# Seven block products in place of eight for the last eight chunks of an up projection

## The chip, the cores and the metric

The kernel runs on one core of a Trainium2 chip, as one program. The metric is device time in microseconds (us) of one execution. The engines are called as the profile calls them: PE (TensorE, the matmuls), PEld (its weight loads), DVE (VectorE), ACT (ScalarE), POOL (GpSimd) and SP (SyncE, which issues most transfers).

## The reference

Two transformer blocks over 512 tokens of width 1024, all in float32. The part around the change is the convolutional feed-forward of the first block:

```
def conv_ffn(x, w_up, conv_w, conv_b, w_down):
    u = causal_dwconv(x @ w_up, conv_w, conv_b)   # 3 taps along the tokens
    g, val = jnp.split(u, 2, axis=-1)             # 2 x 2816 columns
    return (jax.nn.gelu(g) * val) @ w_down
```

Before it stand a mixer and a cross attention, after it a second block with four mixers, an output projection (`out2`) and an MLP, `square(relu(h @ w1)) @ w2` (`m1` and `m2`, hidden width 4096).

## The kernel before

**Work.** Every large product is cut into chunks of one 128x1024 weight tile (512 KB). SP loads chunk after chunk into four stage buffers. Each chunk is split into a rounded part `whi` (ACT, line 1973) and a rest `wlo` (DVE, line 2491); the activations likewise into `xh` and `xl`. A product is then three matmuls: high times high, high times low, low times high. There are seven places for split chunks, so a split runs at most seven chunks ahead of its use.

**A plain up chunk** (`feat`, lines 1509 to 1511) makes 128 features for 512 tokens in one PSUM bank: 8 parts of the contraction x 3 matmuls of 512 columns, 24 matmuls. There are 44: gate and value of each of 22 feature tiles in turn. Behind each chunk ACT copies the bank into `U` (2234) and makes the last tap with bias from the bank (2237); DVE adds two taps (2863, 2866). Behind the gate's taps ACT makes the gelu (2241), behind the value's DVE multiplies the two into `hid1` (2874).

**Seven block products.** `down`, `m2` and the last 24 of 32 tiles of `m1` already use the seven products of a 2x2 block scheme: contraction, features and tokens are halved, and seven products of sums of quarters take the place of eight. In `m1` a group is four chunks' worth of features; its seven products are called, in their order, r2, t11, r1, r3, t12, r4, t22 (`M1_KINDS`). Each is 24 matmuls of 256 columns (1739 to 1741). Between them: after r2 ACT copies the bank away ("taken", 2063); after t11 DVE makes v, which t12 waits for; after r1 DVE makes w (3048) and ACT writes it back ("seed", 2067), which r4 waits for; after r3 DVE makes c22 and c21 (3052, 3054), and t22 waits for c21. Sums of the activations (r1, r2, r3) live in three of the seven places for split chunks (`keep`), given back (`give`) as the last group's r2, r1 and r3 are done. The sums of weight quarters are made in DRAM by transfers of 1 MB that POOL issues one after the other (`add_up`, from the list `ORDER`; `at(n)` names the chunk behind which the n-th may start).

**Order.** A planner (`Plan`) writes one list of steps; each engine takes its own steps out of it in that order, with semaphores between engines. `pump` emits splits until the places are full. Nothing on an engine's queue overtakes.

**The down stage** (`seven`, lines 1713 to 1715) begins with product 0, whose activations are in `first`; products 1 to 3 need x_from 1 to 3 (ACT 2012, DVE 2525), products 4 to 6 need x_from 4 to 6, emitted behind the last chunk's steps. Each product is 12 matmuls of 512 columns. In the last up chunk a semaphore `half` tells after half its matmuls that x_from 1 to 3 may overwrite `xh`.

The plan's loop over the up chunks, before:

```
        for j in self.feat("up", 2 * NF1):
            if j == 2 * NF1 - 1:
                self.seven_ahead("down")
            self.step("up", j // 2, j % 2)
            self.out(("up", j), "up_y", j + 1)
            if j % 8 == 7 and j < 8 * GROUPS["down"]:
                self.combine("down", "r1", j // 8)
                self.combine("down", "r3", j // 8)
            if j == 17:
                self.seven_first("down")
```

## Time and profile before

| | us |
|---|---|
| median of 3 runs | 1231.41 (1231.21 to 1232.08) |
| the profiled execution | 1231.81 |
| its span, first to last instruction | 1230.0 |
| PE busy in it | 1222.7 |
| DVE busy | 899.3 |
| ACT busy | 652.9 |
| last eight up chunks | 569.89 to 613.41 |
| the 42 block products of `m1` | 950.88 to 1071.83 |

Starts in rows are in us from the span's start. A matmul row's own length is a modelled one and overlaps the next; the distance between starts is what PE spends on it. The same holds for ACT and DVE, where an instruction starts a little before the one ahead of it has ended.

### The profile page before, as it was taken

How to read it: one execution, taken by the hardware profiler on the slowest of the kernel's cores; microseconds unless marked ns; L12 is line 12 of the kernel's file. 1: busy time of each engine (PE TensorE's matmuls, PEld its weight loads, DVE VectorE, ACT ScalarE, POOL GpSimd, SP SyncE). 2: the span in 40 equal slices, each digit the busy share in tenths (PEclk: the TensorE clock that was granted, in tenths of full speed). 3: DMA queues.
4: the chain of work that ended last, by engine and by line, in shares of the span. 5: the costliest groups of instructions: out<-in, count | busy, mean ns of one | idle time of the engine just before them, and what ended most of it. 6: DMA issues, size and time to landing. Idle time of an engine off the chain costs nothing.

```text
span 1230.0 us, 17180 instructions
## 1 busy us (share of the span) xinstructions
PE 1222.7 (99%) x6662; PEld 1050.5 (85%) x6662; DVE 899.3 (73%) x1281; ACT 652.9 (53%) x1078; POOL 56.0 (5%) x80
## 2 busy tenths in 40 slices
PE   9999999999999999999999999999999999999998
PEld 9887898898889888888888899778898999988886
DVE  6778888576568656555588587887687777887886
ACT  5565654244546444444465464669354544665654
POOL 0000012000000000000000000000000000000000
PEclk9999999999999999999999999999999999999999
DMA  8445478837635787878676429776736789776562
GB/s 296 150 139 192 161 265 226 283 116 210 185 107 188 209 236 208 198 241 202 212 246 181 139 69 259 207 194 191 248 104 159 265 271 265 256 220 190 173 213 78
DMA packets 63976, 244.53 MB, mean 199 GB/s; under 512 B 6900, under 2 KB 14580, under 8 KB 54424
## 3 DMA queue, kind: packets, MB, share of 16 engines
q1 hardware_dynamic: 53096, 167.55, 40.6%
q0 software_dynamic: 10368, 75.50, 24.9%
q8 instruction: 53, 0.87, 0.3%
q10 hardware_dynamic: 432, 0.39, 0.1%
q14 instruction: 27, 0.22, 0.1%
HBM read 235.55 MB, written 81.26 MB: 258 GB/s over the span
## 4 chain that ended last, share of the span: by engine, by line
PE 99%; DMA 0%; DVE 0%; ACT 0%; issue 0%; DVEq 0%
PE bank L1509 15%; PE bank L1510 15%; PE bank L1511 15%; PE bank L1713 6%; PE bank L1715 6%; PE bank L1714 6%; PE bank L1740 3%; PE bank L1741 3%; PE bank L1739 3%; PE bank L1654 2%; PE bank L1658 2%; PE bank L1653 2%; PE bank L1656 2%; PE bank L1655 2%; PE bank L1657 2%; PE bank L1790 1%
## 5 line engine op out<-in xcount | busy, mean ns | idle before, releaser
L2491 DVE TENSOR_TENSOR wlo<-stage,whi 128x1024 fp32r<-128x1024 f32 (+1 forms) x276 | 332.8, 1212 | 113.5 <-ACT whi L1973 112.4
L1509 PE MATMUL bank<-xh,whi 128*128 128x512 f32 (+1 forms) x944 | 339.4, 360 | 0.2 <-issue 0.2
L1510 PE MATMUL bank<-xl,whi 128*128 128x512 f32 (+1 forms) x944 | 335.5, 355 | 0.0
L1511 PE MATMUL bank<-xh,wlo 128*128 128x512 f32 (+1 forms) x944 | 335.5, 355 | 0.0
L1973 ACT CAST whi<-stage 128x1024 fp32r<-128x1024 f32 (+1 forms) x276 | 284.9, 1039 | 78.5 <-PE bank L1715 27.3
L1509 PEld LDWEIGHTS bank<-xh,whi 128*128 128x128 f32 x944 | 178.5, 189 | 29.9 <-issue 5.3
L1511 PEld LDWEIGHTS bank<-xh,wlo 128*128 128x128 f32 x944 | 178.5, 189 | 25.1
L1510 PEld LDWEIGHTS bank<-xl,whi 128*128 128x128 f32 x944 | 178.6, 189 | 24.4 <-issue 0.2
L1715 PE MATMUL bank<-whi,xl 128*128 128x512 f32 x328 | 127.7, 389 | 0.0
L1714 PE MATMUL bank<-wlo,xh 128*128 128x512 f32 x328 | 127.7, 389 | 0.0
L1713 PE MATMUL bank<-whi,xh 128*128 128x512 f32 x328 | 127.7, 389 | 0.0
L1715 PEld LDWEIGHTS bank<-whi,xl 128*128 128x128 f32 x328 | 61.6, 188 | 12.8
L1714 PEld LDWEIGHTS bank<-wlo,xh 128*128 128x128 f32 x328 | 61.6, 188 | 12.8
L1713 PEld LDWEIGHTS bank<-whi,xh 128*128 128x128 f32 x328 | 61.6, 188 | 12.7
L2863 DVE SCALAR_TENSOR_TENSOR R<-R,par 128x512 f32<-128x512 f32 x44 | 33.1, 752 | 53.2 <-ACT R L2237 53.2
L2234 ACT COPY R<-bank 128x512 f32<-128x512 f32 x44 | 25.8, 587 | 82.4 <-PE bank L1511 82.4
L2525 DVE TENSOR_TENSOR xl<-R,xh 128x512 fp32r<-128x512 f32 x92 | 61.7, 686 | 10.5 <-ACT xh L2012 9.6
L2012 ACT CAST xh<-R 128x512 fp32r<-128x512 f32 x70 | 42.4, 616 | 36.2 <-DVE R L3086 20.1
L1741 PE MATMUL bank<-xh,wlo 128*128 128x256 f32 x192 | 54.4, 283 | 0.0
L1739 PE MATMUL bank<-xh,whi 128*128 128x256 f32 x192 | 54.4, 283 | 0.0
L1740 PE MATMUL bank<-xl,whi 128*128 128x256 f32 x192 | 54.4, 283 | 0.0
L2915 DVE SCALAR_TENSOR_TENSOR R<-R,par 128x512 f32<-128x512 f32 x60 | 41.7, 746 | 1.6 <-ACT R L2280 1.3
(408 smaller groups left out, 2017.7 us busy)
## 6 DMA issues: line engine op xcount, KB each, us to landing
stage<-in_W_m SPq DMA_DIRECT2D x50, 512.0 KB, 4.2
stage<-in_W_up SPq DMA_DIRECT2D x44, 512.0 KB, 4.4
m_a<-in_W_m POOLq DMA_DIRECT2D x14, 1024.0 KB, 8.2
m_b<-in_W_m POOLq DMA_DIRECT2D x14, 1024.0 KB, 7.6
stage<-in_W_in_a SPq DMA_DIRECT2D x19, 512.0 KB, 4.4
stage<-in_W_down SPq DMA_DIRECT2D x18, 512.0 KB, 4.3
stage<-in_W_out SPq DMA_DIRECT2D x16, 512.0 KB, 5.3
m_c<-in_W_m POOLq DMA_DIRECT2D x7, 1024.0 KB, 6.1
```

Source lines behind the costliest of these rows:

```text
L1509: e.matmul(b[:, cols], hi[:, k, :], xh[:, k, cols], start=(k == 0), stop=False)
L1510: e.matmul(b[:, cols], hi[:, k, :], xl[:, k, cols], start=False, stop=False)
L1511: last = e.matmul(b[:, cols], lo[:, k, :], xh[:, k, cols], start=False, stop=(k == 7))
L1713: e.matmul(b[:], x[:, c], hi, start=new, stop=False, skip_group_check=True)
L1714: e.matmul(b[:], x[:, c], lo, start=False, stop=False, skip_group_check=True)
L1715: last = e.matmul(b[:], z[:, c], hi, start=False, stop=end, skip_group_check=True)
L1739: e.matmul(o, hi[:, k, w], x[:, k, :], start=(new and f == 0 and k == 0), stop=False, skip_group_check=True)
L1740: e.matmul(o, hi[:, k, w], z[:, k, :], start=False, stop=False, skip_group_check=True)
L1741: last = e.matmul(o, lo[:, k, w], x[:, k, :], start=False, stop=(k == 3), skip_group_check=True)
L1973: e.copy(whi[:, plan.place[i], 0:width(i)], stage[:, s, 0:width(i)]).then_inc(S["w_hi"])
L2491: e.tensor_tensor(wlo[:, plan.place[i], c], stage[:, i % NSTAGE, c], whi[:, plan.place[i], c].bitcast(F32), ALU.subtract).then_inc(S["w_lo"])
L2525: e.tensor_tensor(lo, source_of(name, k), hi.bitcast(F32), ALU.subtract).then_inc(S["x_lo"])
```

## The change

The last 8 of the 44 plain up chunks become two groups of seven block products (`UP_PLAIN` = 36, 50 chunks in all), with the code of `m1` made general (`feat_seven`, `feat_taken`, `feat_seed`, `feat_combine`). The convolution behind them works on two feature tiles at once: three quarters come by an ACT copy out of the banks (`up_quarter`), the fourth by c22; after r4 ACT makes the value's last tap (`up_y` 1), after t22 the gate's (`up_y` 0), from `U` in SBUF; DVE's taps for the value follow t22 (`up_taps` 1), and those for the gate, the gelus and the multiplications (`up_done`) follow the next group's r2, or t22 itself in the last group. Sums of `x` for r1 to r4 are made beside plain chunks 8 to 15 and 32 to 34 (and r4's rounding after the first r2), and three places are kept for them from chunk 32 on. The weight sums grow from 72 to 80 transfers, in another order of start, with the d sums of `m2` last. x_from 1 to 3 of `down` wait for the second last block product in place of `half`. Behind `out2`, one of two splits moves from ahead of the last tile's norm to behind the turn of tile 2.

```diff
+GROUPS = {"up": 2, "down": 4, "m1": 6, "m2": 8}
+UP_PLAIN = 2 * NF1 - 4 * GROUPS["up"]
+FEATS = {"up": [(kind, g) for g in range(GROUPS["up"]) for kind in M1_KINDS], "m1": M1_SEVEN}
+ORDER = [o for o in ORDER if (o[0], o[2][0]) != ("m2", "d")] + [o for o in ORDER if (o[0], o[2][0]) == ("m2", "d")]
...
             if t == 3:
                 self.used += 5
-                self.pump(2)
+                self.pump(1)
...
             if t >= 2:
                 self.turn(name, t - 1)
+            if t == 3:
+                self.pump(1)
...
-        for j in self.feat("up", 2 * NF1):
-            if j == 2 * NF1 - 1:
-                self.seven_ahead("down")
+        self.up_x = self.x
+        for j in self.feat("up", UP_PLAIN):
...
+            if 8 <= j < 12:
+                self.combine("up", ("t21", "t22", "t11", "t12")[j - 8])
+            elif 12 <= j < 16:
+                self.combine("up", ("r1", "r3", "r2", "r4")[j - 12])
+            elif j == 17:
                 self.seven_first("down")
+            elif UP_PLAIN - 4 <= j < UP_PLAIN - 1:
+                self.sum_kept("up", ("r2", "r1", "r3")[j - UP_PLAIN + 4])
+        for i, (kind, g) in enumerate(FEATS["up"]):
+            self.up_seven(i, kind, g)
...
+    def sum_kept(self, name, kind):
+        self.keep((name, kind))
+        self.step("x_sum", name, kind)
+        self.x_split(name, kind)
+
+    def feat_seven(self, name, i, kind, g, last):
+        if kind not in NEW_BANK:
+            self.fill(name, g, kind)
+        self.need()
+        self.step("seven_feat", name, i)
+        self.used += 1
+        if kind in ("r1", "r2", "r3") and g == last:
+            self.give((name, kind), "mm", CHUNK0[name] + PLAINS[name] + i + 1)
+
+    def up_seven(self, i, kind, g):
+        last = GROUPS["up"] - 1
+        self.feat_seven("up", i, kind, g, last)
+        if kind == "r2":
+            self.copy("up", "taken", g)
+            self.step("feat_taken", "up", g)
+            if g == 0:
+                self.step("x_sum", "up", "r4")
+                self.x_split("up", "r4")
+            else:
+                self.pump()
+                self.up_done(g - 1)
+        elif kind == "t11":
+            self.combine("up", "v", g)
+        elif kind == "r1":
+            self.combine("up", "w", g)
+            self.out(("up", g, "r1"), "combined", self.combined)
+            self.copy("up", "seed", g)
+            self.step("feat_seed", "up", g)
+        elif kind == "r3":
+            self.combine("up", "c22", g)
+            self.combine("up", "c21", g)
+        else:
+            if (kind, g) == ("t22", last):
+                self.seven_ahead("down")
+            n = ("t12", "r4", "t22").index(kind)
+            self.pump()
+            self.step("up_quarter", n, g)
+            self.out(("up", g, ("t11", "r2", "r3")[n]), "up_u", UP_PLAIN + 3 * g + n + 1)
+            if n:
+                self.step("up_y", g, 2 - n)
+            if n == 2:
+                self.step("up_taps", g, 1)
+                if g == last:
+                    self.up_done(g)
+        self.pump()
+
+    def up_done(self, g):
+        self.step("up_taps", g, 0)
+        self.step("up_gelu", g)
+        self.step("up_mult", g)
...
-                if name == "down" and k < 4:
-                    q.wait_ge(S["half"], 3)
-                elif name == "m2" and k < 4:
+                if name in SEVEN and k < 4:
                     q.wait_ge(S["mm"], CHUNK0[name] - 1)
...
+            def up_taps(g, r):
+                for i in range(2):
+                    c, u = UP_PLAIN // 2 + 2 * g + i, U[i][r]
+                    y, w = (hid1[:, c, :] if r else ygs[i]), 22 * r + c
+                    q.wait_ge(S["up_y"], UP_PLAIN + 4 * g + (1 if r else 3) + i)
+                    e.scalar_tensor_tensor(out=y, in0=u[:, 0:512], scalar=P("fcw", w), in1=y, op0=ALU.mult, op1=ALU.add
+                                           ).then_inc(own.inc())
+                    after()
+                    e.scalar_tensor_tensor(out=y, in0=u[:, 1:513], scalar=P("fcw", 44 + w), in1=y, op0=ALU.mult,
+                                           op1=ALU.add).then_inc(S["up_t" if r else "up_c"])
...
-                if n < 43:
-                    return CHUNK0["up"] + 2 + 8 * (n - 17) // 5
-                if n < 61:
-                    return CHUNK0["in2_c"] + 1 + (n - 43)
-                if n < 64:
-                    return CHUNK0["m1"] + 3 + 2 * (n - 61)
-                return CHUNK0["m1"] + PLAIN + 2 + 4 * (n - 64)
+                if n < 40:
+                    return CHUNK0["up"] + 2 + 3 * (n - 17) // 2
+                if n < 58:
+                    return CHUNK0["in2_c"] + 1 + (n - 40)
+                if n < 62:
+                    return CHUNK0["m1"] + 2 + 2 * (n - 58)
+                if n < 72:
+                    return CHUNK0["m1"] + PLAIN + 2 + 4 * (n - 62)
+                return CHUNK0["m2"] + 1 + 4 * (n - 72)
```

## Rows read from the trace of the kernel before

**Rows 1.** The page: PE's busy time, and the granted clock by fortieths of the span

```profile
PE 1222.7 (99%) x6662; PEld 1050.5 (85%) x6662; DVE 899.3 (73%) x1281; ACT 652.9 (53%) x1078; POOL 56.0 (5%) x80
...
PEclk9999999999999999999999999999999999999999
```

**Rows 2.** The longest wait of PE in the span: total, times, longest

```profile
PE bank L1952 <- DVE R L2564: 1.2, 1, 1.2
```

**Rows 3.** PE's timeline: first matmul of the stretches named in the prediction

```profile
569.89 0.39 PE L1509 MATMUL bank<-xh,whi 128*128 128x512 f32 x1
...
613.41 0.39 PE L1713 MATMUL bank<-whi,first 128*128 128x512 f32 x1
...
950.88 0.28 PE L1739 MATMUL bank<-whi 128*128 128x256 f32 x1
...
1071.83 0.40 PE L1713 MATMUL bank<-whi,first 128*128 128x512 f32 x1
```

**Rows 4.** Timeline of ACT, then of DVE, around plain up chunks

```profile
570.09 0.59 ACT L2234 COPY R<-bank 128x512 f32<-128x512 f32 x1 [0.58 <-PE bank L1511]
570.57 0.79 ACT L2237 ACTIVATE R<-bank,par 128x512 f32<-128x512 f32 x1
571.24 1.05 ACT L1973 CAST whi<-stage 128x1024 fp32r<-128x1024 f32 x1
578.47 0.63 ACT L2241 ACTIVATE R<-R 128x512 f32<-128x512 f32 x1 [1.68 <-DVE R L2866]
...
576.89 0.75 DVE L2863 SCALAR_TENSOR_TENSOR R<-R,par 128x512 f32<-128x512 f32 x1 [2.04 <-ACT R L2237]
577.68 0.75 DVE L2866 SCALAR_TENSOR_TENSOR R<-R,par 128x512 f32<-128x512 f32 x1
```

**Rows 5.** Timeline of ACT, then of DVE, in the last block group of `m1`

```profile
1055.23 2.00 ACT L1973 CAST whi<-stage 128x1024 fp32r<-128x1024 f32 x2
1061.23 0.59 ACT L2067 COPY bank<-R 128x512 f32<-128x512 f32 x1 [2.49 <-DVE R L3048]
...
1056.39 2.36 DVE L2491 TENSOR_TENSOR wlo<-stage,whi 128x1024 fp32r<-128x1024 f32 x2 [0.73 <-ACT whi L1973]
1060.51 0.69 DVE L3048 TENSOR_TENSOR R<-R,bank 128x512 f32<-128x512 f32 x1
1065.18 0.68 DVE L3052 TENSOR_TENSOR R<-R,bank 128x512 f32<-128x512 f32 x1
1065.78 0.69 DVE L3054 TENSOR_TENSOR bank<-bank,R 128x512 f32<-128x512 f32 x1
```

**Rows 6.** Timeline of ACT, then of DVE, where `down` begins

```profile
612.59 1.66 ACT L2012 CAST xh<-R 128x512 fp32r<-128x512 f32 x3
...
619.05 0.68 DVE L2525 TENSOR_TENSOR xl<-R,xh 128x512 fp32r<-128x512 f32 x1
```

**Rows 7.** DMA issues of 612 to 622 us, then the page's: KB, us to landing

```profile
stage<-down_c SPq DMA_DIRECT2D x1, 512.0 KB, 3.2
stage<-in_W_down SPq DMA_DIRECT2D x1, 512.0 KB, 3.4
...
stage<-in_W_up SPq DMA_DIRECT2D x44, 512.0 KB, 4.4
```

**Rows 8.** Windows, busy us by engine: the last up chunks, a group of `m1`

```profile
569.86:613.41 43.55, 43.55 (x194) 36.06 (x193) 24.62 (x29) 20.89 (x30) 3.00 (x5) 1.00 0.75 217
950.90:971.00 20.10, 20.10 (x169) 20.10 (x168) 15.87 (x20) 11.79 (x15) 1.07 (x2) 1.00 0.76 246
```

**Rows 9.** POOL's timeline: the last sums issued beside the up chunks

```profile
569.62 0.81 POOL L3317 DMA_DIRECT2D m_c<-m_a  x1 [9.32 <-DMA m_b<-in_W_m]
578.57 0.83 POOL L3317 DMA_DIRECT2D m_d<-m_c  x1 [8.14 <-DMA m_c<-m_a]
```

**Rows 10.** ACT's timeline at the last tile of `out2`

```profile
899.91 2.00 ACT L1973 CAST whi<-stage 128x1024 fp32r<-128x1024 f32 x2
904.90 0.60 ACT L2413 ACTIVATE R<-bank 128x512 f32<-128x512 f32 x1 [2.99 <-PE bank L1658]
```

More of the change, by code:

```diff
@@ L1139, in m1_seven @@
+    def up_done(self, g):
+        self.step("up_taps", g, 0)
+        self.step("up_gelu", g)
+        self.step("up_mult", g)
+        c = UP_PLAIN // 2 + 2 * g + 2
+        if c % 4 == 0 and c <= 4 * GROUPS["down"]:
+            self.combine("down", "r1", c // 4 - 1)
+            self.combine("down", "r3", c // 4 - 1)
+    def m1_seven(self, i, kind, g):
+        self.feat_seven("m1", i, kind, g, NF2 // 4 - 1)
         if kind == "r2":
             self.copy("m1", "taken", g)
-            self.step("m1_taken", g)
+            self.step("feat_taken", "m1", g)
@@ L1377, in build_program @@
         hid2 = tiles(reg(16, NF2 * 512), NF2)
-        rs = {"down": [tiles(reg(60 + 2 * g, 512), 2) for g in range(4)],
+        rs = {"down": [tiles(reg(kb, 512), 2) for kb in (60, 62, 92, 94)],
               "m2": [tiles(reg(92 + 2 * g, 512), 2) for g in range(2)]
@@ L1460, in build_program, with feat_x @@
         turned = [nc.dram_tensor(f"turned{u}", (128, 1024 if u % 4 else 512), F32, kind="Internal").ap() for u in range(8)]
[L1462 removed]
+        def feat_x(name, kind, lo):
             if kind in ("r1", "r2", "r3"):
[L1464 removed]
+                return tiles((wlo if lo else whi)[:, plan.kept[name, kind][0], :], 4)
             k, c = X_T["t21" if kind == "r4" else kind]
@@ L1521, in feat @@
                 ks = {None: range(8), "front": range(4), "back": range(4, 8)}[part]
-                if (name, j) in LAST_X.values():
-                    by_weights(b, i, cols, range(4)).then_inc(S["half"])
-                    ks = range(4, 8)
                 last = by_weights(b, i, cols, ks)
@@ new lines, in x_sum, with feat_taken @@
+                e.copy(feat_x(name, kind, 0), raw_of(SUM_AT[kind])).then_inc(S["x_hi"])
+            def feat_taken(name, g):
+                q.wait_ge(S["mm"], CHUNK0[name] + PLAINS[name] + FEATS[name].index(("r2", g)) + 1)
+                if name == "up":
+                    if g >= 2:
+                        q.wait_ge(S["combined"], plan.combined_at["up", "c21", g - 2])
+                    else:
+                        q.wait_ge(S["x_lo"], plan.x_at["up", "r3"])
+                e.copy(feat_v[name][:, g % 2, :], bank_of(name, g, "r2")[:]).then_inc(S["taken"])
@@ new lines, in feat_seed, with up_quarter @@
+            def feat_seed(name, g):
+                q.wait_ge(S["combined"], plan.combined_at[name, "w", g])
+                e.copy(bank_of(name, g, "r2")[:], feat_w[name][:, g % 2, :]).then_inc(S["taken"])
+            def up_quarter(n, g):
+                q.wait_ge(S["mm"], CHUNK0["up"] + UP_PLAIN + FEATS["up"].index((("t12", "r4", "t22")[n], g)) + 1)
+                q.wait_ge(S["up_t" if n == 1 else "up_c"], UP_PLAIN // 2 + 2 * g)
+                e.copy(u_of(("t11", "t12", "t21")[n]), tiles(bank_of("up", g, ("t11", "r2", "r3")[n])[:], 2)).then_inc(S["up_u"])
@@ new lines, in up_y @@
+            def up_y(g, r):
+                q.wait_ge(S["up_u"], UP_PLAIN + 3 * g + 3 - r)
+                if r:
+                    q.wait_ge(S["combined"], plan.combined_at["up", "c22", g])
+                else:
+                    q.wait_ge(S["up_h"], UP_PLAIN // 2 + 2 * g)
+                    q.wait_ge(S["x_lo"], plan.x_at["up", "r4"])
+                for i in range(2):
+                    c = UP_PLAIN // 2 + 2 * g + i
+                    e.activation(hid1[:, c, :] if r else ygs[i], U[i][r][:, 2:514], ACT.Identity, bias=P("fcb", 22 * r + c),
+                                 scale=P("fcw", 88 + 22 * r + c)).then_inc(S["up_y"])
@@ L2069, in m1_quarter, with up_gelu @@
+            def up_gelu(g):
+                for i in range(2):
+                    q.wait_ge(S["up_c"], UP_PLAIN // 2 + 2 * g + i + 1)
+                    e.activation(ygs[i], ygs[i], ACT.Gelu_apprx_tanh).then_inc(S["up_g"])
             def m1_quarter(n, g):
-                q.wait_ge(S["mm"], CHUNK0["m1"] + PLAIN + M1_SEVEN.index((("t12", "r4", "t22")[n], g)) + 1)
+                q.wait_ge(S["mm"], CHUNK0["m1"] + PLAIN + FEATS["m1"].index((("t12", "r4", "t22")[n], g)) + 1)
                 e.activation(t_of("m2", ("t11", "t12", "t21")[n], g), tiles(bank_of("m1", g, ("t11", "r2", "r3")[n])[:], 2),
@@ L3044, in m1_combine @@
                     e.tensor_tensor(v, v, b1, ALU.subtract).then_inc(S["combined"])
                 elif kind == "w":
-                    q.wait_ge(S["mm"], done + M1_SEVEN.index(("r1", g)))
-                    q.wait_ge(S["combined"], plan.combined_at["m1", "v", g])
+                    q.wait_ge(S["mm"], done + FEATS[name].index(("r1", g)))
+                    q.wait_ge(S["combined"], plan.combined_at[name, "v", g])
+                    if name == "up" and g >= 2:
+                        q.wait_ge(S["taken"], plan.copied_at["up", "seed", g - 2])
@@ L3056, in m1_last, with up_mult @@
+            def up_mult(g):
+                for i in range(2):
+                    c = UP_PLAIN // 2 + 2 * g + i
+                    q.wait_ge(S["up_t"], c + 1)
+                    q.wait_ge(S["up_g"], c + 1)
+                    e.tensor_tensor(hid1[:, c, :], ygs[i], hid1[:, c, :], ALU.mult).then_inc(S["up_h"])
             def m1_last(g):
```

150 lines of the change are left out of this document (75 added, 75 removed).

## The prediction

> **What bounds the kernel now.** I read the page first: PE is busy 1222.7 us of 1230.0 and its granted clock is full in all forty slices [rows 1]. Next the waits of PE: the longest of all is 1.2 us, at the start [rows 2]. So the time is the sum of the matmuls, and any other engine counts only when it makes PE wait; the reader should then look for how near the others are to that. The windows say it: in a group of m1's block products DVE is busy 15.87 of 20.10 us, ACT 11.79 [rows 8]. The timelines give each instruction's pace [rows 4 to 6], and it is these that decide here.
>
> **What PE saves.** Eight plain up chunks last from 569.89 to 613.41, 43.52 us, 5.44 a chunk, 0.2267 a matmul of 512 columns. m1's 42 block products last from 950.88 to 1071.83, 120.95 us, so 2.88 each, 0.120 a matmul of 256 columns [rows 3]. Two groups are 14 x 2.88 = 40.32 us: PE saves **3.20 us** (0.26%), if nothing makes it wait.
>
> A rule of the Trainium skill gives another price (TensorE: Matmul & The Clock Gate, "Wait — 56ns, not 53.3ns?"): a warm matmul costs its columns at 2.4 GHz plus about 2.5 ns. By it the saving would be an estimated 192 x 215.8 - 336 x 109.2 ns = 4.7 us, and my result 1.5 us lower; these rows pay some 13 ns beyond the columns, so the row's price stands.
>
> **What stands between the products.** Paces, start to start. DVE: a wlo 1.14 (two end 2.36 after the first begins, one lasts 1.22), an addition of 512 columns 0.60 (1065.18 to 1065.78) [rows 5], a tap 0.79 (576.89 to 577.68) [rows 4]. ACT: a whi 0.95 [rows 5], a bank copy 0.48 to 0.50, a last tap 0.67 (570.57 to 571.24) [rows 4], an x cast 0.52 (three in 1.66) [rows 6]. Hand-over: 0.20 from PE's last matmul to ACT [rows 3, 4], 1.16 from a whi's start to its wlo's, 0.72 from w to the seed [rows 5], 0.79 from the last tap to the gelu (577.68 to 578.47) and, by its 0.63 length, 0.66 from gelu to multiplication (an estimate) [rows 4].
>
> A group asks of DVE 7 wlo (7.98), v, w, c22, c21 (2.40), 8 taps (6.32) and 2 multiplications (1.20): 17.9 us of 20.16, where the last eight plain chunks left it busy 24.62 of 43.55 [rows 8]. On average that fits. The order decides whether it fits in time. I follow both queues from the first block product (0 = its start), with products at 2.88.
>
> *First group.* v is ready at 7.9 (due 11.5, when t12 starts), c21 at 13.8 (due 17.3). PE doesn't wait. But ACT can take the last quarter only after t22, and the value's taps stand on DVE behind t22's wlo, though their inputs are ready by then.
>
> *Second group, from 20.16.* The eleventh split's whi starts at 20.39 (ACT has just ended the value's last taps), its wlo at 21.55. DVE has stood idle from 19.8. Value taps 22.69 to 25.85. Then r2's step: as r2's place is given back, two splits are due, to 28.13; then the four gate taps to 31.29; the first multiplication; the second waits for the second gelu, 31.95; v starts at 32.54 and ends at 33.2. t12 was due at 11 x 2.88 = 31.68: **PE 1.6 late**. Then wlo 33.14, w 34.28, seed 35.00. r1 gives back another place, so two more splits, which on ACT stand behind the seed: whi at 35.5, wlo 36.7 and 37.8, c22 38.96, c21 39.56 to 40.25. t22 would start at 39.05 now: **another 1.3**. down starts at 43.2, not 40.32.
>
> *Start of down.* r3's two splits and t12's, r4's follow on ACT. The load into a stage buffer is issued when the wlo four chunks earlier is done, here 37.9, and takes 3.2 to 3.4 us alone, 4.4 in the middle of the up stage [rows 7]. So that whi starts at 41.2 to 42.4; behind it a quarter's copy, a whi, a copy and two last taps, then x_from 1 at 45.5 to 46.7, whose DVE part ends 1.35 later. down's product 1 is due at 45.9: **1.0 to 2.2**. x_from 4 has more ahead of it on DVE: x_from 1 to 3, a wlo, eight taps and two multiplications with a gelu between: it is ready 2.6 after product 4 is due: **2.6**. Behind it DVE needs 1.74 to 2.35 a product (wlo, x, at times a sum) against 2.72, so it catches up. Before the change the same x_from 4 ended at 619.7, 4.6 ahead of its product at 613.41 + 4 x 2.72 [rows 3, 6].
>
> Sum of waits: 6.5 with the fastest loads, 7.7 with the slowest. I take 3.5 us a load, nearer the lone ones, since no sum is left then (below): **6.8 us**.
>
> A bound from below, with no idling on DVE at all from 21.55: eleven wlo 12.5, sixteen taps 12.6, eleven additions 6.6, and x_from 4's own 0.69 are 32.4, so 54.0 at best, due 40.32 + 10.88 = 51.2. At least 2.8 us are lost by DVE's work alone. From above: all four waits with loads of 4.4.
>
> That DVE and ACT don't overtake is what all this rests on. The Trainium skill says the same (TensorE page, "Architectural detail": both are strict FIFO queues).
>
> **The other edits.** (a) Sums of x: 8 operations of DVE of 1024 columns beside plain chunks 8 to 15, and three casts and three subtractions beside 32 to 34, one per 5.44 us chunk, where DVE has more than 2 us free [rows 8]; no splits are due while three places go. Nothing; without that cover about 1.2 each. (b) x_from 1 to 3 freed by the second last product instead of `half`: the permission comes 2.88 ahead of down, as early as half a chunk was; nothing by itself. (c) Sums in DRAM: one in about 9 us (569.62 to 578.57) [rows 9], and 23 now want to start beside the plain chunks, one in 8.2 us; they run late, by some 20 us into the first group, and slow loads that are four products ahead. Nothing; for m2 each d sum starts 20 to 29 chunks ahead of its use. If one came late, PE would wait for its 9 us transfer. (d) out2: the second split stood in 2.99 us in which ACT waited for PE [rows 10], and its chunk is used three half chunks (8.6 us) and more later. PE waits in neither place [rows 2]: nothing, from a loss of 1 us at most if the split is late. (e) The last tap is read from SBUF rather than from PSUM: up to 0.13 a piece less on ACT, 0.3 in all on the chain to x_from 1.
>
> **Result.** Profiled execution: 1231.81 - 3.20 + 6.8 = 1235.4, with 1.8 outside the span as now. It stands 0.4 above the median of the runs, so the median becomes **1235.0 us**, slower by 0.29%. Without the third and fourth of its waits it would be 1231.1; own range 1233.5 to 1236.
>
> **Rivals.** (1) *DVE is late but never idle, the loads and ACT never in the way*: 2.8 us lost, 1231.0, the same. For it: the fit on average; against it: every idle stretch above is a wait for a whi that stands behind something. (2) *DVE keeps up*: faster, 1228.2. This is so if x_from 4 is ready by 51.2 and c21 by 37.4, that is if the taps find the idle stretches, such as that from 19.8 to 21.5 in which the value's taps could begin. It needs a DVE order other than I read from the plan. For it: m1's groups have no wait, with 2.5 us to spare at the last c21 (1066.5 against 41 x 2.88 + 950.88 = 1068.96) [rows 3, 5]; against it: up adds 6.3 us of taps in front of v. (3) *PE's clock drops in the waits*: every granted clock is full here, the longest idling 1.2 us [rows 1, 2]; one wait of 2.6 is longer than the trace shows. At 1.2 GHz a down product takes 5.44; three of them add 8 us, of which later waits hide a part: about 1240. The skill's page on TensorE ("What's actually happening") holds that the clock is released by activity and throttled by idling, which would make such a wait dearer; no row here shows it. (4) *The sums of m2's d come late*: 1240 or more.
>
> **Chances.** Forecast 0.55; (1), with values up to 1233.9 in which part of the waits is gone, 0.23; (2) 0.13; (3) 0.06; (4) 0.03. A measurement of this kernel tells 0.2% (2.5 us) from no change. Slower by more 0.63, within 0.24, faster 0.13. The range reaches from rival 1, a little below, to past the slowest loads with something for the clock: 1230.3 to 1237.5.
>
> **What the profile would show.** Right: PE's waits of 1.6 and 1.3 us in the second group, on DVE's v and c21, and of 1 to 3 us on x_from 1 and 4 in down, none in the first group; 2.88 a product; DVE with eight taps ahead of x_from 4. Wrong: a PE without waits there, taps in another place, or a granted clock below full after 600 us.

## The result, and the profile after

The changed kernel takes 1242.85 us (median of 5 executions, 1241.48 to 1244.55) against 1231.41 before: a ratio of 1.0093 [1.0081, 1.0104], slower by a little under 1%, clear of the noise. The profiled execution has a span of 1241.6 us, 11.6 more than before. The forecast was 1235.0: its sign was right, its size some 8 us too small.

The page of the changed kernel, PE's busy time and the clock by fortieths. In the forty slices little shows; PE's digit is 8 in two slices where it was 9, and the clock's digit, 9 for anything from 90% up, is the same:

```profile
PE 1223.8 (99%) x6806; PEld 1056.1 (85%) x6806; DVE 922.7 (74%) x1307; ACT 663.5 (53%) x1090; POOL 61.5 (5%) x88
...
PE   9999999999999999999899999999999999899998
...
PEclk9999999999999999999999999999999999999999
```

The waits of PE from 565 us on (total, times, longest), where the kernel before had none over 0.2:

```profile
PE bank L1779 <- DVE wlo L2583: 3.8, 1, 3.8
PE bank L1779 <- DVE xl L2617: 2.1, 1, 2.1
PE bank L1804 <- DVE bank L3157: 1.7, 2, 1.0
PE bank L1779 <- issue: 1.6, 1, 1.6
PE bank L1804 <- DVE R L3139: 1.3, 1, 1.3
```

PE's timeline has the places. L1804 to L1806 are block products by features (up, m1), L1779 to L1781 those of down and m2, L3139 is v, L3157 c21:

```profile
601.05 0.28 PE L1806 MATMUL bank<-whi,wlo 128*128 128x256 f32 x1
602.65 0.36 PE L1804 MATMUL bank<-xh,whi 128*128 128x256 f32 x1 [1.32 <-DVE R L3139]
...
608.36 0.28 PE L1806 MATMUL bank<-xh,wlo 128*128 128x256 f32 x1
609.65 0.36 PE L1804 MATMUL bank<-xh,whi 128*128 128x256 f32 x1 [1.02 <-DVE bank L3157]
...
617.07 0.47 PE L1779 MATMUL bank<-whi,xh 128*128 128x512 f32 x1 [1.57 <-issue]
...
625.12 0.39 PE L1781 MATMUL bank<-whi,xl 128*128 128x512 f32 x1
627.57 0.47 PE L1779 MATMUL bank<-whi,xh 128*128 128x512 f32 x1 [2.06 <-DVE xl L2617]
...
628.44 0.63 PE L1779 MATMUL bank<-whi,xh 128*128 128x512 f32 x1
628.87 0.63 PE L1780 MATMUL bank<-wlo,xh 128*128 128x512 f32 x1
...
631.43 0.48 PE L1780 MATMUL bank<-wlo,xh 128*128 128x512 f32 x1
```

A wait costs more than its bracket says: from start to start less the usual pitch (0.12 and 0.227), the four cost 1.48, 1.17, 1.73 and 2.22, in all 6.60. Each is followed by one interval that is some 0.08 too long (602.65 to 602.84), in all 0.3. Behind the last, ten intervals take 3.86 us (627.57 to 631.43) instead of 2.27: another 1.6. The windows show why: the clock of that stretch was for the most part at the lower of its two levels, 1.2 GHz. The second window has the wait of 3.8 us that ends at 1084.45, and behind it the same happens again, for another 1.6 us:

```profile
628.00:632.00 4.00, 4.00 (x13) 3.10 (x12) 3.07 (x6) 3.94 (x6) 0.00 (x0) 0.57 0.00 0
...
1080.00:1095.00 15.00, 11.20 (x42) 8.76 (x42) 14.31 (x20) 10.36 (x16) 0.54 (x1) 0.89 0.76 271
```

By stage, first matmul to first matmul, with the marks of [rows 3]: PE reaches the first block product 0.39 earlier (569.50), all of which lies ahead of the up stage and differs from execution to execution (the first up chunk starts between 380.2 and 382.1 in the profiles of this case). Up's end takes 43.09 instead of 43.52. From down's first product (612.59) to the first of m1's blocks (955.86) it is 343.27 instead of 337.47, 5.80 more, all of it in down. m1's blocks take 121.88 instead of 120.95, m2 up to its last matmul 157.81 instead of 152.12 (1223.95 before, 1235.55 after). The sum of the five differences is the 11.6.

So there are two sites. One is where I looked: +5.4 net at the second group and down's start, of which 1.6 is the clock. The other, +6.6, is the end of m1 and the start of m2, where I had priced the moved sums at nothing: 0.9 at the last t22 (a wait of 0.71), 4.0 at m2's product 1 (products are counted from 0) and 1.6 of clock behind it.

At the first site, ACT waits twice for a load ahead of x_from 1 (the profile names no releaser for PE's wait at product 1; the first xl of x_from 1 ends at 616.97, just ahead of 617.07). Then DVE makes eight taps and two multiplications between a wlo and the xl of x_from 4:

```profile
610.40 1.05 ACT L2038 CAST whi<-stage 128x1024 fp32r<-128x1024 f32 x1 [1.72 <-DMA stage<-down_a]
612.65 1.05 ACT L2038 CAST whi<-stage 128x1024 fp32r<-128x1024 f32 x1 [0.71 <-DMA stage<-down_c]
...
618.34 1.23 DVE L2583 TENSOR_TENSOR wlo<-stage,whi 128x1024 fp32r<-128x1024 f32 x1 [0.17 <-ACT whi L2038]
619.48 0.75 DVE L3164 SCALAR_TENSOR_TENSOR R<-R,par 128x512 f32<-128x512 f32 x1
...
626.74 0.68 DVE L2617 TENSOR_TENSOR xl<-R,xh 128x512 fp32r<-128x512 f32 x1
```

ACT's timeline at the second site, in the changed kernel:

```profile
1066.41 1.05 ACT L2038 CAST whi<-stage 128x1024 fp32r<-128x1024 f32 x1 [4.20 <-DMA stage<-m_d]
1069.41 0.59 ACT L2136 COPY bank<-R 128x512 f32<-128x512 f32 x1 [1.96 <-DVE R L3145]
1069.94 2.94 ACT L2038 CAST whi<-stage 128x1024 fp32r<-128x1024 f32 x3
1077.91 1.05 ACT L2038 CAST whi<-stage 128x1024 fp32r<-128x1024 f32 x1 [5.02 <-DMA stage<-m_b]
```

ACT stands in a split and waits for its load, longer than any product lasts. POOL's timeline names what the loads share the DMA with. Two of m2's sums run there, and a third is issued at 1080.95; the last sum before the change was issued at 1037.73:

```profile
1054.46 0.83 POOL L3440 DMA_DIRECT2D m_b<-in_W_m  x1 [10.89 <-PE bank L1806]
1066.21 0.81 POOL L3440 DMA_DIRECT2D m_c<-m_a  x1 [10.92 <-DMA m_b<-in_W_m]
```

DMA issues from 1048 to 1085 us (KB each, median us to landing), the kernel before first, without a sum in flight from about 1048 on:

```profile
stage<-m_a SPq DMA_DIRECT2D x4, 512.0 KB, 3.8
stage<-m_c SPq DMA_DIRECT2D x3, 512.0 KB, 4.3
stage<-m_b SPq DMA_DIRECT2D x3, 512.0 KB, 4.7
stage<-m_d SPq DMA_DIRECT2D x1, 512.0 KB, 3.1
```

and the kernel changed:

```profile
stage<-m_b SPq DMA_DIRECT2D x3, 512.0 KB, 5.9
stage<-m_a SPq DMA_DIRECT2D x3, 512.0 KB, 7.0
stage<-m_c SPq DMA_DIRECT2D x3, 512.0 KB, 6.9
m_b<-in_W_m POOLq DMA_DIRECT2D x1, 1024.0 KB, 11.3
...
stage<-m_d SPq DMA_DIRECT2D x1, 512.0 KB, 9.5
```

The loads from `in_W_m` in the same stretch went from 3.9 to 4.9. No load waited for its sum: from 1050 us on the only thing for which SP held a weight load back was a stage buffer, that is the wlo that frees it (total, times, longest):

```profile
SPq L3301 <- DVE wlo L2583: 138.1, 59, 6.2
```

### The profile page after: what moved, and what is told of

The parts are those of the page before. It is cut to its first block, busy times and chain, and to the rows that moved or that the text cites. A ratio compares the mean times of both kernels' runs of the same rounds, so it can differ in the third digit from the quotient of the medians.

```text
span 1241.6 us, 17554 instructions
## 1 busy us (share of the span) xinstructions
PE 1223.8 (99%) x6806; PEld 1056.1 (85%) x6806; DVE 922.7 (74%) x1307; ACT 663.5 (53%) x1090; POOL 61.5 (5%) x88
## 4 chain that ended last, share of the span: by engine, by line
PE 93%; DVE 2%; DMA 2%; ACT 1%; issue 1%; DVEq 0%; ACTq 0%
PE bank L1578 14%; PE bank L1579 13%; PE bank L1580 13%; PE bank L1779 6%; PE bank L1780 6%; PE bank L1781 6%; PE bank L1806 3%; PE bank L1805 3%; PE bank L1804 3%; PE bank L1720 2%; PE bank L1724 2%; PE bank L1721 2%; PE bank L1719 2%; PE bank L1723 2%; PE bank L1722 2%; DVE wlo L2583 1%
## 5 line engine op out<-in xcount | busy, mean ns | idle before, releaser
L1578 PE MATMUL bank<-xh,whi 128*128 128x512 f32 (+1 forms) x880 | 314.2, 357 | 0.2 <-issue 0.2
L1579 PE MATMUL bank<-xl,whi 128*128 128x512 f32 (+1 forms) x880 | 310.3, 353 | 0.0
L1580 PE MATMUL bank<-xh,wlo 128*128 128x512 f32 (+1 forms) x880 | 310.2, 353 | 0.0
L1578 PEld LDWEIGHTS bank<-xh,whi 128*128 128x128 f32 x880 | 166.3, 189 | 27.5 <-issue 5.3
L1580 PEld LDWEIGHTS bank<-xh,wlo 128*128 128x128 f32 x880 | 166.3, 189 | 22.8
L1779 PE MATMUL bank<-whi,xh 128*128 128x512 f32 x328 | 129.2, 394 | 7.4 <-DVE wlo L2583 3.8
L1781 PE MATMUL bank<-whi,xl 128*128 128x512 f32 x328 | 129.0, 393 | 0.0
L1779 PEld LDWEIGHTS bank<-whi,xh 128*128 128x128 f32 x328 | 62.3, 190 | 21.7 <-issue 4.4
L1804 PE MATMUL bank<-xh,whi 128*128 128x256 f32 x256 | 72.7, 284 | 3.0 <-DVE bank L3157 1.7
L1781 PEld LDWEIGHTS bank<-whi,xl 128*128 128x128 f32 x328 | 62.2, 190 | 13.1
L1805 PE MATMUL bank<-xl,whi 128*128 128x256 f32 x256 | 72.4, 283 | 0.0
L1806 PE MATMUL bank<-xh,wlo 128*128 128x256 f32 x256 | 72.4, 283 | 0.0
L2955 DVE SCALAR_TENSOR_TENSOR R<-R,par 128x512 f32<-128x512 f32 x36 | 27.0, 751 | 37.9 <-ACT R L2328 37.9
L1805 PE MATMUL bank<-wlo,whi 128*128 128x256 f32 x192 | 54.3, 283 | 0.0
```

The costliest lines, as they stand in the source:

```text
L1578: e.matmul(b[:, cols], hi[:, k, :], xh[:, k, cols], start=(k == 0), stop=False)
L1579: e.matmul(b[:, cols], hi[:, k, :], xl[:, k, cols], start=False, stop=False)
L1580: last = e.matmul(b[:, cols], lo[:, k, :], xh[:, k, cols], start=False, stop=(k == 7))
L1779: e.matmul(b[:], x[:, c], hi, start=new, stop=False, skip_group_check=True)
L1781: last = e.matmul(b[:], z[:, c], hi, start=False, stop=end, skip_group_check=True)
L1804: e.matmul(o, hi[:, k, w], x[:, k, :], start=(new and f == 0 and k == 0), stop=False, skip_group_check=True)
```

## The experiments

Fifteen kernels ran; each ratio is against the kernel before on the same chip. Theory one: the end of m1 is the sums' timetable alone. Theory two, for the first site: only the order of DVE's queue is at fault, since on average the work fits. Its rival: the work itself is too much there.

### The sums respaced

Eight sums beside m1's block groups as before the change, the rest later in m2.

```diff
-                if n < 72:
+                if n < 70:
                     return CHUNK0["m1"] + PLAIN + 2 + 4 * (n - 62)
-                return CHUNK0["m2"] + 1 + 4 * (n - 72)
+                if n < 72:
+                    return CHUNK0["m2"] + 3 + 4 * (n - 70)
+                return CHUNK0["m2"] + 11 + 3 * (n - 72)
```

> The changed kernel with another timetable of the weight sums alone: beside m1's block groups only the first 8 of the 10 sums (the last behind product 30 instead of 38 of them), the two others and the d sums of m2 during m2. Theory: the changed kernel loses at two places independent of each other; the second, at the end of m1 and the start of m2, comes from loads of 7 to 9.5 us beside sums of m2 while splits fall due in pairs. So the waits of 0.7 and 3.8 us there and the slow matmuls behind them go, the places in up and down stay: 1242.85 - 6.6 = 1236.2 us (1235.5 to 1237.5). Rival: the waits there come from elsewhere (later phase after the stall in down, the split moved behind out2): 1241 to 1244.

Measured: 1236.26 us (1.0045 [1.0028, 1.0062]), span 1233.5. Both waits of the second site are gone, the four of the first stand (1.4, 1.0, 1.6, 2.1), and 0.4 is new at down's product 16. As expected by theory one, the median is 6.6 us lower. Of the profiles, m1's blocks are back at 120.95 and m2 is at 152.55, together 6.2 us less; the profiled span is 8.1 less, as here the clock also stayed full behind the wait of 2.06 at product 4:

```profile
627.00:631.00 4.00, 4.00 (x19) 3.32 (x18) 3.06 (x5) 3.81 (x6) 0.00 (x0) 1.00 0.15 59
```

### The kernel before, with its sums late

```diff
+ORDER = [o for o in ORDER if (o[0], o[2][0]) != ("m2", "d")] + [o for o in ORDER if (o[0], o[2][0]) == ("m2", "d")]
...
                 if n < 64:
-                    return CHUNK0["m1"] + 3 + 2 * (n - 61)
-                return CHUNK0["m1"] + PLAIN + 2 + 4 * (n - 64)
+                    return CHUNK0["m1"] + PLAIN + 2 + 4 * (n - 54)
+                return CHUNK0["m2"] + 1 + 4 * (n - 64)
```

(with the sums ahead of these spread over the earlier stages so that 54 are out when m1's groups begin)

> The kernel before with the late timetable alone: 72 sums, no block groups in up, the m2 d sums last, 10 sums beside m1's block groups up to behind product 38 and 8 beside m2. Theory: the place at the start of m2 shows in it too, with waits on wlo there and none in up and down: 1231.4 + 6.6 = 1238 us (1234 to 1239.5; how long a load takes beside a sum depends on where the two meet). Rival (the new place is a consequence of the block groups in up): 1231.4, no wait.

Measured: 1238.51 (1.0059 [1.0044, 1.0075]), span 1235.3. Its two waits from 540 us on, in m1's last group and in m2's start:

```profile
PE bank L1710 <- DVE wlo L2488: 3.1, 1, 3.1
PE bank L1736 <- DVE bank L3051: 0.3, 1, 0.3
```

No block product in up, and a wait in the same place (m2's product 1), with the same slow clock behind it: the second site needs no group in up. Theory one is shown from both sides. Which of the moved sums does it, the last two beside m1's groups or the first beside m2, these two kernels don't separate.

### DVE's order, on top of the change and with the sums respaced

v, w and the seed moved ahead of the first group's last taps (a); the last group's taps moved behind down's products 1 and 3 (b).

```diff
+            if g:
+                self.up_done(g - 1)          # (a) in r1's step, no longer in r2's
...
-                self.step("up_taps", g, 1)
-                if g == last:
-                    self.up_done(g)
+                if g < last:
+                    self.step("up_taps", g, 1)
...
+            if name == "down" and i == 1:    # (b)
+                self.step("up_taps", GROUPS["up"] - 1, 1)
+            if name == "down" and i == 3:
+                self.up_done(GROUPS["up"] - 1)
```

Both, with the sums of the change:

> The changed kernel with another order of the vector queue alone: in the second up group v, w and the seed stand ahead of the first group's gate taps, gelus and multiplications, and the last group's taps, gelus and multiplications stand behind down's products 1 and 3 instead of ahead of x_from 4. Theory: the four waits in up and down and the slow clock behind them go, so that place gives the 3.2 us of the matmuls instead of taking 5.4: 1242.85 - 8.6 = 1234.2 us (1233 to 1236.5). Rival (the vector engine's sum of work, or the loads, hold PE up whatever the order): at least 2.8 us of waits stay there, 1237 or more.

Both, with the sums respaced:

> Both together: the timetable of the first experiment and the order of the third. Theory: no wait at either place, the matmuls' saving is all that is left: 1231.4 - 3.2 = 1228.2 us (1227.8 to 1229.5). Rival (work or loads hold PE up whatever the order): 1231 or more.

(b) alone and (a) alone, with the sums respaced:

> The kernel changed, with the two summing transfers respaced as in the first experiment (that one took 1236.3) and only the last group's four-tap sets moved behind down's products 1 and 3; v and w stay where the change has them. DVE's work is only moved to a later due time. If DVE has no slack there (the theory now): the wait at product 4 (2.06) goes, the waits at t12 and t22 (1.36, 1.02) stay, and a new wait of 2 to 4 us stands at the 17th product of down (about 660 us): 1236 to 1238. If the order is what costs: product 4's wait goes and nothing takes its place, 1233.5.

> The kernel changed, with the respaced sums, and only v, w and the seed of a group moved ahead of the first group's last taps, gelu and product. If DVE's work is what is short: the wait at t12 (1.36) goes, those of t22, x_from 1 and product 4 grow by about as much in all, 1235 to 1237, with no new wait at 660 us. If the order is what costs: 1234.9.

Measured: 1244.94, 1238.50, 1239.58 and 1241.52 us (ratios 1.0107, 1.0059, 1.0066, 1.0063; the last between 1.0036 and 1.0090). The first compares with the changed kernel's 1242.85, the other three with the respaced sums' 1236.26: no median is better, though with (a) alone the median hides a gain (below). The waits of the second one:

```profile
PE bank L1781 <- DVE R L3215: 4.3, 1, 4.3
PE bank L1781 <- issue: 1.5, 1, 1.5
PE bank L1806 <- DVE bank L3159: 1.1, 1, 1.1
```

The waits at t12 and at product 4 are gone, as they should be, and a new one of 4.3 us stands at 661 us, down's product 16, on v of down (L3215). It comes with (b) alone too, at the same 4.3. DVE's timeline just ahead of it shows a queue that does nothing but its regular work and never gets ahead:

```profile
655.16 1.23 DVE L2585 TENSOR_TENSOR wlo<-stage,whi 128x1024 fp32r<-128x1024 f32 x1 [0.33 <-ACT whi L2040]
656.30 0.69 DVE L2619 TENSOR_TENSOR xl<-R,xh 128x512 fp32r<-128x512 f32 x1
656.91 1.22 DVE L2585 TENSOR_TENSOR wlo<-stage,whi 128x1024 fp32r<-128x1024 f32 x1
658.04 0.68 DVE L2619 TENSOR_TENSOR xl<-R,xh 128x512 fp32r<-128x512 f32 x1
658.64 1.22 DVE L2585 TENSOR_TENSOR wlo<-stage,whi 128x1024 fp32r<-128x1024 f32 x1
659.78 1.28 DVE L3215 TENSOR_TENSOR R<-R,bank 128x512 f32<-128x512 f32 x2
```

The windows of the kernel before had said so, had I cut them there (busy us of PE, PEld, DVE, ACT, POOL): 

```profile
624.00:635.00 11.00, 11.00 (x50) 9.09 (x50) 9.98 (x13) 7.39 (x10) 0.00 (x0) 1.00 0.89 308
...
657.00:668.00 11.00, 11.00 (x50) 9.13 (x49) 10.07 (x14) 5.58 (x8) 0.00 (x0) 1.00 0.43 114
...
690.00:712.00 22.00, 22.00 (x98) 18.21 (x97) 10.99 (x21) 7.22 (x13) 0.00 (x0) 1.00 0.18 49
```

The first two windows are the fullest; from 613.41 to 690 us DVE is busy 65.2 of 76.6, and up to 657, where v falls due, 37.3 of 43.6. The group's last taps and multiplications are 7.5 us, so by these numbers 1.2 us are missing at product 16 even if DVE never idled (an estimate). What the last group leaves behind on DVE can't be worked off there, only handed to the next due point. For (b), theory two falls.

For (a) it holds. The wait at t12 is gone and the others did not grow (1.1, 1.6, 2.1): from the first block product to down's the profile has 41.63 us where the respaced sums alone have 43.14, and from there to m1's blocks the same (342.40 and 342.35). That is the whole 1.5 us of the wait at t12. It is the other branch of what I expected, in which the order is what costs (1234.9), that came. The times hide it: the executions were 1234.39 to 1242.85, and the profile, the slowest of them, had 5.8 us at m2's product 32, behind ACT idling 4.9 us for a load of one of m2's d sums. The two fastest executions, 1234.39 and 1235.50, fit a kernel without that wait; no trace of them is kept.

### Less work for DVE

One group instead of two (tiles 20 and 21), then both groups with half of DVE's taps; this second kernel leaves out a part of the convolution.

```diff
-UP_PLAIN = 2 * NF1 - 4 * GROUPS["up"]
+UP_GROUPS = 1
+UP_PLAIN = 2 * NF1 - 4 * UP_GROUPS
```

> The kernel changed, with the respaced sums, and one group of seven block products (tiles 20 and 21) in place of two; the 40 chunks ahead are plain. PE saves 1.6 instead of 3.2. If the backlog that each group leaves on DVE is the cause: the waits at t12 and t22 go, of the 3.6 at down's products 1 and 4 some 2 to 3.3 stay, 1231.5 to 1233.5. If only the start of down costs (its taps and x splits at once, however many groups): 3.6 and the 1.4 at half clock stay, 1234.9. If one group is free: 1229.8.

```diff
-                    e.scalar_tensor_tensor(out=y, in0=u[:, 0:512], scalar=P("fcw", w), in1=y, op0=ALU.mult, op1=ALU.add
-                                           ).then_inc(own.inc())
-                    after()
```

> The kernel changed, with the respaced sums, and one of the two taps left out of the convolution of the last four pairs of tiles (those of the two groups), so its output isn't the reference's: 8 instructions of 0.75 us fewer on DVE, 6.0 in all, and nothing else changed, not the order or any wait but these. If DVE's work is the cause: of the 6.4 us of waits of PE at the second group and at down's start at most 1.5 are left, nothing at half clock, 1228.2 to 1230. If the waits come from the order and from latencies of ACT's chain: 1235 to 1236.

Measured: 1233.87 (1.0023 [1.0009, 1.0036]) and 1231.40 (1.0011 [0.9993, 1.0030]). The waits of the second:

```profile
PE bank L1779 <- issue: 1.7, 1, 1.7
PE bank L1804 <- DVE bank L3157: 0.4, 1, 0.4
```

Six us of taps fewer, and of 6.1 us of waits 4.0 are gone: all of those at t12 and product 4, and 0.6 of the 1.0 at t22. The time came out 1.4 above the bound that I gave, as product 1's 1.7 us stay. These are not DVE's work: x_from 1 stands on ACT behind splits that wait for their loads (1.76 and 0.83 us idle at 608.73 and 611.09 in that kernel) and behind two quarters and two last taps, as the prediction had it. One group alone shows the same parting: no wait in the group, 0.8 at product 1, 2.1 at product 4 (and 0.4 us over the range that I gave).

### The groups where DVE has room

In the kernel before, DVE was busy 24.62 of 43.55 us beside the last eight plain chunks [rows 8]. So the groups go ahead of them: tiles 14 to 17 are the groups', 18 to 21 plain again. The plain chunks need x whole, so r4's sum takes a fourth kept weight place instead of lying over x, and three are left. The last plain chunk is in halves again. With (a), and the sums respaced as above.

```diff
+UP_AFTER = 8
-UP_PLAIN = 2 * NF1 - 4 * GROUPS["up"]
+UP_PLAIN = 2 * NF1 - 4 * GROUPS["up"] - UP_AFTER
...
-        for j in self.feat("up", UP_PLAIN):
+        for j in self.feat("up", 2 * NF1):      # skips the groups' eight
+            if j == 2 * NF1 - 1:
+                self.seven_ahead("down")
...
+            if j == UP_PLAIN - 1:
+                self.pump()
+                for i, (kind, g) in enumerate(FEATS["up"]):
+                    self.up_seven(i, kind, g)
```

> The whole computation. The two groups stand ahead of the last eight plain chunks instead of behind all of them: 28 plain, 14 block products, 8 plain (the plain chunks behind need the input whole, so the sum for r4 lies in a fourth kept weight place and three are left for weights); v and w ahead of the last group's taps; the last plain chunk in halves as in the kernel before, the sums respaced. If the cause is DVE's backlog that meets down's start, where DVE has no slack: the eight plain chunks (43.5 us, DVE busy about 25) absorb it, down starts as in the kernel before, PE keeps most of its 3.2: 1228 to 1229.5. If the groups cost PE the same wherever they stand (DVE, ACT or the places beside them): waits of 2 to 6 us in and just behind the groups, 1231 to 1234.

With `UP_AFTER = 4`:

> As the run before, with four plain chunks behind the groups instead of eight (32, 14, 4): 21.8 us in which DVE has about 9 to spare. By the backlog of 7.5 us that the last group leaves this is just enough: 1228 to 1230. If slack isn't what matters: the same as the run before, whatever that gives.

Measured: 1231.84 (1.0016 [1.0003, 1.0029]) and 1236.30 (1.0049 [1.0031, 1.0067]). Both are over what I expected (1229.5 and 1230 at most). With eight behind, down has no wait left and takes its 337.47 us again; 2.1 us stand in the second group at t22, 3.0 in m2 at product 32. With four behind, down's product 1 waits 3.9 for a split: I had expected 9 us of slack to do for a backlog of 7.5, and they don't. But that kernel doesn't show DVE short of time: from 589 to 611 us it is busy only 15.6 of 22, with DVE and ACT waiting for one another in turn, while three sums run beside the chunks (issued at 589.60, 601.24 and 610.10) and loads from two of down's sum arrays take 6.5 and 8.4 us in the median. And both kernels change more than the place: the last chunk is in halves again, r4's sum has a place of its own, and no sum is issued beside the groups after their first product. Which of these took product 1's wait away is not shown.

Beside these two stood the kernel before with the edit at out2's last tile alone:

```diff
-                self.pump(2)
+                self.pump(1)
...
+            if t == 3:
+                self.pump(1)
```

> The kernel before with the one edit at out2's last tile alone: one split there, the other behind the norm. The prediction priced it at nothing: 1231.4. If it matters, by at most the one split that it moves, 1.2 us: 1230.2 to 1232.6.

Measured: 1231.12 (1.0000 [0.9990, 1.0009]): nothing, as predicted in (d).

### What was left: a timetable, and one order

Two sums go beside down's last products, eight beside m1's groups, m2's d from its product 5 on (a new timetable, T2). In the third kernel of this set, the first group's gate taps, gelu and product also stand behind c22 and c21 of the second group instead of ahead of them.

```diff
-                if n < 58:
-                    return CHUNK0["in2_c"] + 1 + (n - 40)
-                if n < 62:
-                    return CHUNK0["m1"] + 2 + 2 * (n - 58)
+                if n < 42:
+                    return CHUNK0["down"] + 26 + 4 * (n - 40)
+                if n < 60:
+                    return CHUNK0["in2_c"] + 1 + (n - 42)
+                if n < 64:
+                    return CHUNK0["m1"] + 2 + 2 * (n - 60)
                 if n < 72:
-                    return CHUNK0["m1"] + PLAIN + 2 + 4 * (n - 62)
-                return CHUNK0["m2"] + 1 + 4 * (n - 72)
+                    return CHUNK0["m1"] + PLAIN + 2 + 4 * (n - 64)
+                return CHUNK0["m2"] + 5 + (0, 3, 7, 10, 14, 17, 21, 24)[n - 72]
...
             self.combine("up", "c21", g)
+            if g:
+                self.step("up_taps", g - 1, 0)  # the gelu and product follow in t12's step
```

The change with T2:

> The kernel changed with only its timetable of summing transfers changed: two of them go beside down's last products (DMA share 0.18 there in the kernel before), so that eight stand beside m1's block products as in the kernel before, and the eight of m2's d begin at m2's product 5 instead of after 11. If the respaced timetable of the first experiment was itself late in some executions (stage loads of m2's d waiting for their sum at about 1155 us, 3 to 6 us of wait of PE), the spread of the times narrows and only up's and down's waits stay: 1234.5 to 1235.5. If the new places hold the loads of the sums' neighbours up: over 1236.5, with waits in down's last products or in m2.

The groups ahead of eight plain chunks with T2, then with the order too:

> The kernel with the groups ahead of the last eight plain chunks, with the same new timetable of sums. There the wait of 3.05 at m2's product 32 was of its profile, 2.11 at the second group's t22 too. If the first belongs to the timetable it goes, the second stays: 1228.5 to 1230, and the slow executions of up to 1238 are gone. If PE's time is set by something else in m2: no change, 1231.8.

> As the run before, with the first group's gate taps, gelu and product moved behind v, w, c22 and c21 of the second group (they stood ahead of c22 and c21). If the 2.11 at t22 is those 4 taps and 2 products (4.4 us) ahead of c21 on DVE: it goes or falls under 0.7, and the plain chunks behind absorb them: 1227 to 1228.5. If DVE's total is what counts here too: a wait of the same size comes up at the first plain chunks behind, and the time is that of the run before.

Measured: 1236.38 (1.0039 [1.0026, 1.0052]); 1232.54 (1.0011 [1.0003, 1.0020]); 1229.50 (0.9986 [0.9977, 0.9994]). The changed kernel gains nothing over the first respacing and still has 2.0 us in m2, against what I expected. In the other two, the 2.1 at t22 stays with T2 and is gone with the order, and nothing takes its place: from the first block product to down's it is 83.86 us instead of 87.69, which is the wait's 2.3 and some 1.5 of clock behind it. Both are over the ranges that I gave (1230 and 1228.5 at most), and the third's executions still spread from 1227.15 to 1234.01 though its profile has no wait of PE at all from 540 us on.

Last, four sums beside down's products 20 to 32 instead of two, and so six in m2 instead of eight:

```diff
-                if n < 42:
-                    return CHUNK0["down"] + 26 + 4 * (n - 40)
+                if n < 44:
+                    return CHUNK0["down"] + 20 + 4 * (n - 40)
...
+                return CHUNK0["m2"] + 5 + 4 * (n - 74)
```

> As the run before (1229.5, a profile of 1226.5 without any wait of PE behind up's start, and executions up to 1234), with four instead of two sums beside down's products 20 to 32 and six instead of eight in m2, the last there at m2's product 25 instead of 29. If m2's sums are what makes executions differ: a median of 1227.5 to 1228.5 and few over 1230. If the sums now hold up loads in down (where DVE has no slack to product 28): over 1230, with waits in down. If the spread is from elsewhere: 1229.5 as before.

Measured: 1228.28 us (1227.17 to 1228.93), ratio 0.9974 [0.9963, 0.9984], span 1226.3. Its eight executions lie within 1.8 us, where the twelve of the kernel ahead of it had four above 1230, and this version is faster than both kernels, by 0.26% against the one before. Its windows, columns as in [rows 8], from the groups to down's start and on to 690 us:

```profile
525.00:609.00 84.00, 84.00 (x530) 76.49 (x529) 64.84 (x76) 51.46 (x69) 3.52 (x5) 1.00 0.73 216
609.00:690.00 81.00, 81.00 (x359) 67.05 (x359) 67.12 (x82) 51.38 (x71) 2.43 (x4) 1.00 0.78 255
```

PE is never idle and the clock is full. The first block product starts at 525.87 and down at 609.73: 83.86 us for 14 x 2.88 + 8 x 5.44 = 83.84. All behind it, down, m1's blocks and m2, takes what it took in the kernel before (337.47, 120.95 and 152.12).

## Why the prediction was right and wrong

**PE's saving, right.** 3.20 us by [rows 3]. The last kernel pays 83.86 us where sixteen plain chunks would take 87.04, and its median is 3.0 below that of the kernel before beside it.

**The four waits, right in place and nearly in size.** Forecast: v 1.6, c21 1.3, x_from 1 1.3, x_from 4 2.6, in all 6.8. Measured from start to start: 1.48, 1.17, 1.73, 2.22, in all 6.60, and 0.3 in the intervals behind them. The two queues, followed instruction by instruction, gave this; busy shares (15.87 of 20.10 in m1's groups, which never wait [rows 8]) would have given none. That DVE's work stands behind three of the four is shown by the kernel without half of the taps.

**The clock, a term that the sum had at nothing.** It stood only in rival 3, at 3 products of half speed and a chance of 0.06, and as a sign of being wrong (a clock below full after 600 us), which came. In the changed kernel's profile it fell twice, behind the waits of 2.06 and 3.80, for some 3 us each, and cost 1.6 each: a fifth of the rival's price a time, 3.2 us in all, and part of the outcome, not an alternative to it. It does not belong to a wait as such: the same 2.06 us left it full in the kernel with respaced sums.

**The failed step: edit (c), "Sums in DRAM: ... Nothing".** It is the largest error, 6.6 of the 8 us (the 1.6 of clock behind its wait included); the clock at the first site is 1.6 more, and the small rest nearly cancels: 0.3 behind the waits, 0.2 less in the waits themselves, 0.4 earlier at the up stage. Without this step the profiled execution would have come out near 1236.8, inside the range. I followed the 23 sums of the up stage (PE waited nowhere beside them, and the last was issued at 570.10, earlier than I had it) and asked whether the sums came late for their use. I did not ask what the later ones would run beside. Eight sums more, and 62 of them ahead of m1's groups where there had been 64, meant ten beside the groups instead of eight, and two of them over the last group, where splits fall due in pairs and m2's x casts are queued behind them on the same ACT. Loads from the sums' arrays, 3.1 to 4.7 us in the median, became 5.9 to 9.5. Rival 4 (1240 or more, a chance of 0.03) has the number but not the mechanism: it named the sums of m2's d as late, and no load waited for a sum; it was loads beside sums. That it needs no group in up is shown by the kernel before with its sums late.

**The prediction's edits (a), (b), (d), (e), right as far as seen.** No wait before the second group; (d) measured alone at 1.0000. The sums of x, (a), and the tap read from SBUF, (e), were not tried alone. For (b), the missing `half`, product 1's wait is ACT's queue, but an x_from 1 placed earlier in it wasn't tried, so how much of its 1.7 the lost half chunk explains stays open.

**Open.** What makes executions of the kernels with eight or ten sums in m2 differ was seen in three profiles only, each time at m2's product 32 (5.8 us at 1168, 3.0 at 1160, 2.0 at 1165), behind splits that waited for a load of m2's d. With two sums fewer in m2 and two more in down no such execution was among eight; the mechanism between is argued, and eight are few against the four slow ones of twelve. Why the clock falls behind one wait and not behind a like one no run here shows.

## What to carry to other kernels

A stage with slack on average may have none at its edge: cut the windows of the other engines where the moved work comes due, and just behind it, before trusting the mean. When a backlog moves from one due point to the next under a reordering, as with (b), the work is too much there, and the place to look for is a stretch with room behind it. Where nothing new stands behind the moved work, as with (a) and with the taps behind c21, the order was at fault. Judge both by the stage in the trace, as a wait elsewhere can hide the gain in the time of the whole kernel. And when a list of background transfers grows, write down for each of them what it will run beside, to the end of the program: the loss came 450 us after the edit.

## What the runs showed of the hardware that I had not expected

- Behind some waits of PE, and within the longest, the granted clock fell, and matmuls of 512 columns ran at about half clock for some 3 us: 0.63 us long, 0.43 apart, granted clock 0.57 in the window of 628 to 632 us. It cost 1.6 us each time (2.06 and 3.80 in the changed kernel). The length of the wait alone didn't decide it. Behind waits of 2.00 to 2.11 us the clock fell in four profiles (the changed kernel, one group, the groups ahead of eight chunks with T2, the change with T2 at 1165 us) and stayed full in four (respaced sums, these with (a), the change with T2 at 627 us, the groups ahead of eight chunks with respaced sums). It fell behind one of 1.89 (both orders with the sums of the change, 615 us) and stayed full behind one of 2.74 (the same kernel, 661 us) and one of 3.05 (the groups ahead of eight chunks, 1160 us). Behind waits of up to 1.7 us it never fell.
- A wait costs PE some 0.16 us more than the profile's bracket says, since the bracket starts at the modelled end of the matmul before, which lies that much behind the usual pitch (0.28 against 0.12, 0.39 against 0.227). The interval behind the first matmul is some 0.08 too long on top (0.19 and 0.31).
- Loads of 512 KB from m2's sum arrays had medians of 5.9 to 9.5 us in a stretch in which transfers of 1 MB between DRAM arrays ran one after the other, and of 3.1 to 4.7 without them.
